# Loading the prompt rows by feature columns and the first weight piece in two halves at the start of a decoder step

## The chip, the cores and the metric

The kernel runs on one core of a Trainium2 chip. The metric is the device time of one launch in microseconds. Three runs of the kernel before gave 911.23, 910.31 and 910.13 us, median 910.31 us.

## What is computed

One layer of a decoder for 512 prompt tokens and 8 sample tokens, 1024 features each, all in float32. The first step, which the change touches, is the input projection, a product of all 520 token rows with a weight matrix of 5376 columns; the kernel computes its first 2048 columns (pooling input, keys, memory query, queries) in one stage of its own:

```
z = x @ w_in        # x: 512 prompt rows and 8 sample rows, 1024 features
q, k, v, u, cq, gates = split(z)
```

After it come rotary embedding, windowed attention with sinks, causal pooling, cross-attention into 256 memory tokens, a gated merge, a layer norm, a mixture of 16 experts (top 2 inside the best group of 4) and a second layer norm. None of these is changed.

## The kernel before

The program is written out engine by engine, with semaphores between the engines; every engine runs its instructions in the order of the text. The change and the steps argued on lie in the first 33 us and a little behind them.

**Loads (SP, from L369).** SP issues all early loads on one hardware queue, in this order: the identity matrix (64 KB, 512-byte rows; `id_in`), the prompt rows in four blocks of 128 tokens (L372, each 512 KB with rows of 4 KB; all four count `x_in`), the 8 sample rows (L373, 32 KB, also `x_in`), the first two weight pieces of `wz` (L380, 1 MB each, into `raw[0]` and `raw[1]`, `raw_in`), the memory rows `mtok` (L384, 1 MB, `m_in`), and then the constants, parameters, pooling and router weights (L385 to L390). At L392 and L393 SP waits until all nine transposed tiles are split, then loads the pooling state (L394), and then piece after piece of `wz` into the two `raw` buffers, each as soon as the piece before it in that buffer is split (L397 to L400).

**Transposes (PE, L1020 to L1031).** PE waits for the identity and for all five loads of `x_in` together (L1021). It transposes the sample rows (8 small transposes, L1023, one increment of `xt_ps`), and then for each block `k` of 128 features the four blocks of 128 tokens into PSUM bank `4 + k % 4` (L1030, four transposes of 128 by 128 for each `k`, one increment). From `k` = 4 on it waits until the bank is free again, that is until ACT and DVE have both read it (L1027, L1028).

**Splits (ACT L586 to L608, DVE L1658 to L1679).** A float32 value is split into a high part in the reduced type `fp32r` and a low part. For the activations ACT copies the PSUM bank to `xhi` (L607, 512 columns; L587 for the sample rows), and DVE subtracts it from the bank to give `xlo` (L1677; L1659). For a weight piece ACT copies `raw` to `whi` (L595, 2048 columns) and DVE gives `wlo` (L1669). Both engines do the sample rows first, then `k` = 0 to 3, then the whole weight piece 0, then `k` = 4 to 7, then piece 1.

**Projection (PE, `z_piece` at L1059, `product` at L1033).** A piece of `wz` holds two output tiles of 128 columns (the halves `u` = 0 and 1, 1024 elements of each partition). Each tile takes 48 matmuls of 260 columns: for two token halves and eight feature blocks the three products hi*hi (L1041), lo*hi (L1042) and hi*lo (L1043). `z_piece(0)` waits for `lo_split` 1, the low part of the whole piece, and its first 24 matmuls wait block by block for `xhi` and `xlo` (L1039, L1040). ACT copies each finished tile to `z` (L618 for tile 0, L620 for tile 1), and then splits the piece that has landed in the buffer that is free. There are eight pieces; the transposes of `mtok` come behind the eighth (L1084).

## Time and profile before

| | |
|---|---|
| median of three runs | 910.31 us |
| the profiled execution: device time | 910.77 us |
| its span, first to last instruction | 908.6 us |
| PE busy | 837.1 us (92% of the span) |
| DVE, ACT, POOL busy | 530.1, 434.5, 170.5 us |
| mean granted clock of TensorE | 0.956 |
| first instruction of PE | 9.87 us after the span's start |
| first matmul of the projection | 19.28 us |

The span is counted from the first instruction of any engine, and 2.2 us of the device time lie outside it. The chain of waits follows the instruction that ended last back to what released it; what stands on it set the end. The timeline gives the instructions of one engine in order; what stands in brackets is the time that the engine was idle before and what ended it. "PEclk" is the clock that TensorE was granted, 1.00 being 2.4 GHz and 0.50 being 1.2 GHz. The queue of SP lists the issue of a load, not its arrival.

### The profile page before, as it was taken

To read this page: it belongs to the slowest core of one execution; us is meant where nothing else is said; L and a number is where in the kernel's file an instruction comes from. 1 tells how busy PE (TensorE), PEld (TensorE's weight loads), DVE (VectorE), ACT (ScalarE), POOL (GpSimd) and SP (SyncE) were. 2 spreads that over 40 slices of the span, in tenths; PEclk is the share of its full clock that TensorE was granted. 3 is DMA by queue.
4 is the path that set the end of the run, shared out by engine and by line. 5 is a ranking of instruction groups with operands and counts; after the bars stand their busy time and mean duration, and the time that the engine had idled before them with its cause. 6 is when DMAs were issued, how large, how long until landed. Compare 5 with 4: busy or idle time off the path is not lost.

```text
span 908.6 us, 13893 instructions
## 1 busy us (share of the span) xinstructions
PE 837.1 (92%) x5420; PEld 742.1 (82%) x5420; DVE 530.1 (58%) x710; ACT 434.5 (48%) x575; POOL 170.5 (19%) x147
## 2 busy tenths in 40 slices
PE   4999988898997999999999997599999999999990
PEld 4999977787885989999999776487888888888870
DVE  3122255646346333444443434779999999999976
ACT  4222232556356242233223214267888788788753
POOL 0086013222122100000000055411121112111104
PEclk9999999999899699999999999599999999999995
DMA  7422200831012113222223363899999999999953
GB/s 293 150 93 92 92 24 25 297 144 48 24 48 88 47 42 132 88 87 87 87 87 139 103 206 129 298 413 397 400 402 389 388 401 402 381 396 402 361 142 94
DMA packets 38143, 179.80 MB, mean 198 GB/s; under 512 B 3919, under 2 KB 11759, under 8 KB 23854
## 3 DMA queue, kind: packets, MB, share of 16 engines
q1 hardware_dynamic: 32486, 159.22, 46.0%
q0 software_dynamic: 5600, 19.99, 7.9%
q8 instruction: 26, 0.43, 0.2%
q14 instruction: 15, 0.12, 0.0%
q10 hardware_dynamic: 16, 0.03, 0.0%
HBM read 164.65 MB, written 16.89 MB: 200 GB/s over the span
## 4 chain that ended last, share of the span: by engine, by line
PE 87%; DVE 6%; DMA 3%; ACT 2%; issue 1%; SPq 0%; DVEq 0%; POOL 0%; POOLq 0%; ACTq 0%
PE ps L1164 7%; PE ps L1165 6%; PE ps L1541 6%; PE ps L1166 6%; PE ps L1543 6%; PE ps L1542 6%; PE ps L1041 4%; PE ps L1042 4%; PE ps L1043 4%; PE ps L1568 3%; PE ps L1570 3%; PE ps L1569 3%; PE ps L1180 2%; PE ps L1182 2%; PE ps L1181 2%; PE ps L1529 2%
## 5 line engine op out<-in xcount | busy, mean ns | idle before, releaser
L2030 DVE TENSOR_TENSOR elo<-eraw,ehi 128x2048 fp32r<-128x2048 f32 x96 | 218.0, 2291 | 25.6 <-ACT ehi L880 23.7
L880 ACT ACTIVATE ehi<-eraw 128x2048 fp32r<-128x2048 f32 x96 | 183.0, 1916 | 27.2 <-PE ps L1543 15.9
L1541 PE MATMUL ps<-ehi,xethi 128*128 128x512 f32 x256 | 103.1, 403 | 3.7 <-issue 2.4
L1543 PE MATMUL ps<-elo,xethi 128*128 128x512 f32 x256 | 101.0, 394 | 0.0
L1542 PE MATMUL ps<-ehi,xetlo 128*128 128x512 f32 x256 | 100.9, 394 | 0.0
L1041 PE MATMUL ps<-xhi,whi 128*128 128x260 f32 x256 | 73.2, 286 | 2.4 <-DVE wlo L1669 2.4
L1164 PE MATMUL ps<-xhi,whi 128*128 128x260 f32 x256 | 74.5, 291 | 0.0
L1165 PE MATMUL ps<-xhi,wlo 128*128 128x260 f32 x256 | 74.0, 289 | 0.0
L1166 PE MATMUL ps<-xlo,whi 128*128 128x260 f32 x256 | 73.9, 289 | 0.0
L1042 PE MATMUL ps<-xhi,wlo 128*128 128x260 f32 x256 | 73.0, 285 | 0.0
L1043 PE MATMUL ps<-xlo,whi 128*128 128x260 f32 x256 | 72.7, 284 | 0.0
L1836 DVE TENSOR_TENSOR wlo<-late,whi 128x2048 fp32r<-128x2048 f32 (+1 forms) x16 | 34.5, 2158 | 64.4 <-ACT whi L813 64.4
L1669 DVE TENSOR_TENSOR wlo<-raw,whi 128x2048 fp32r<-128x2048 f32 x11 | 25.7, 2333 | 68.2 <-ACT whi L595 68.2
L1541 PEld LDWEIGHTS ps<-ehi,xethi 128*128 128x128 f32 x256 | 48.8, 191 | 16.7 <-DVE elo L2030 3.8
L2381 POOL TENSOR_TENSOR probs<-probs,stat 128x1024 f32<-128x1024 f32 (+1 forms) x20 | 34.4, 1722 | 129.5 <-DVE stat L1759 129.5
L1543 PEld LDWEIGHTS ps<-elo,xethi 128*128 128x128 f32 x256 | 48.6, 190 | 10.4
L676 ACT ACTIVATE probs<-probs,stat 128x256 f32<-128x256 f32 (+1 forms) x80 | 38.0, 476 | 38.7 <-DVE stat L1742 36.2
L1542 PEld LDWEIGHTS ps<-ehi,xetlo 128*128 128x128 f32 x256 | 48.7, 190 | 9.3
L2426 POOL DMA_INDIRECT f_dram<-yout,dest x14 | 28.7, 2051 | 121.3 <-ACT yout L900 121.3
L1568 PE MATMUL ps<-ehi,hthi 128*128 128x512 f32 x128 | 51.4, 401 | 0.0
L1041 PEld LDWEIGHTS ps<-xhi,whi 128*128 128x128 f32 x256 | 48.9, 191 | 2.7 <-DVE wlo L1669 2.7
L1164 PEld LDWEIGHTS ps<-xhi,whi 128*128 128x128 f32 x256 | 50.1, 196 | 0.3 <-issue 0.3
(370 smaller groups left out, 2069.1 us busy)
## 6 DMA issues: line engine op xcount, KB each, us to landing
eraw<-w_gate_in SPq DMA_DIRECT2D x32, 1024.0 KB, 20.3
eraw<-w_up_in SPq DMA_DIRECT2D x32, 1024.0 KB, 20.5
eraw<-w_down_in SPq DMA_DIRECT2D x32, 1024.0 KB, 22.2
raw<-wz_in SPq DMA_DIRECT2D x8, 1024.0 KB, 5.2
late<-wm_in SPq DMA_DIRECT2D x8, 896.0 KB, 4.4
late<-wm_in SPq DMA_DIRECT2D x8, 704.0 KB, 4.0
fraw<-wm_in SPq DMA_DIRECT2D x8, 512.0 KB, 3.5
late<-wo_in SPq DMA_DIRECT2D x4, 1024.0 KB, 4.9
```

Of the source, the lines that this page charges most:

```text
L880: ac.activation(ehi[s % 3][:, :], eraw[s][:, :], ACT.Copy).then_inc(ehi_ok, 1)
L1041: pe.matmul(out, sh, mh[n], start=start and k == 0, stop=False)
L1042: pe.matmul(out, sl, mh[n], start=False, stop=False)
L1043: last = pe.matmul(out, sh, ml[n], start=False, stop=stop and k == len(parts) - 1)
L1164: pe.matmul(out, cols(whi[s], q), mh, start=start, stop=False)
L1165: pe.matmul(out, cols(wlo[s], q), mh, start=False, stop=False)
L1166: return pe.matmul(out, cols(whi[s], q), ml, start=False, stop=stop)
L1541: pe.matmul(ps[:, bank, :], hi[:, k, :], ehi[s[j]][:, w], start=k == 0, stop=False)
L1542: pe.matmul(ps[:, bank, :], lo[:, k, :], ehi[s[j]][:, w], start=False, stop=False)
L1543: last = pe.matmul(ps[:, bank, :], hi[:, k, :], elo[s[j]][:, w], start=False, stop=k == KD - 1)
L1568: pe.matmul(ps[:, bank + h, :], hi[:, f, :], ehi[s[j]][:, w], start=f == 0, stop=False)
L2030: ve.tensor_tensor(elo[s % 3][:, :], eraw[s][:, :], ehi[s % 3][:, :].bitcast(F32), ALU.subtract)\
```

## The change

SP now loads the prompt rows in four blocks of 256 features for all 512 tokens (`columns`, each 512 KB in rows of 1 KB), each with a semaphore of its own, `x_in[0]` to `x_in[3]`. Behind the first two of them comes the first half of weight piece 0 (512 KB, `first_in`), then the sample rows (which now count `x_in[1]`), then the last two blocks, then the second half of piece 0 (`raw_in[0]`), then piece 1. The load of `mtok` moves behind the wait for the transposes and the load of the pooling state.

PE waits for one block of features ahead of every second `k`; ahead of `k` = 2 it waits for 32 on `x_in[1]`, the block and the sample rows. The sample transposes move from the front to `k` = 4, and so do their splits on ACT and DVE. Both of these engines split the first half of piece 0 ahead of `k` = 2 (1024 columns, `first_hi`, `first_lo`), and the second half behind `k` = 7. `z_piece(0)` waits for `first_lo` ahead of its first tile and for `lo_split` 1 ahead of its second. Two semaphores that nothing used are dropped.

```diff
-id_in, con_in, x_in, m_in = sem("id_in"), sem("con_in"), sem("x_in"), sem("m_in")
+id_in, con_in, m_in = sem("id_in"), sem("con_in"), sem("m_in")
+x_in = [sem(f"x_in{c}") for c in range(4)]
+first_in, first_hi, first_lo = sem("first_in"), sem("first_hi"), sem("first_lo")
...
-    for t in range(NB):
-        sp.dma_start(xtok[:, t, :], xp[:, t, :]).then_inc(x_in, 16)
-    sp.dma_start(xsam[:, :], a["x_sample"]).then_inc(x_in, 16)
+
+    def columns(c):
+
+        cols = slice(c * 2 * P, c * 2 * P + 2 * P)
+        sp.dma_start(xtok[:, :, cols], xp[:, :, cols]).then_inc(x_in[c], 16)
+
+    columns(0)
+    columns(1)
+    sp.dma_start(raw[0][:, 0:D], a["wz"][0, :, 0:D]).then_inc(first_in, 16)
+    sp.dma_start(xsam[:, :], a["x_sample"]).then_inc(x_in[1], 16)
+    columns(2)
+    columns(3)
+    sp.dma_start(raw[0][:, D:PW], a["wz"][0, :, D:PW]).then_inc(raw_in[0], 16)
...
-    for n in range(2):
-        piece(n, a["wz"][n], PW, True)
-    sp.dma_start(mtok[:, :, :], a["mem_prompt"].rearrange("(t p) d -> p t d", p=P)).then_inc(m_in, 16)
+    piece(1, a["wz"][1], PW, True)
...
+    sp.dma_start(mtok[:, :, :], a["mem_prompt"].rearrange("(t p) d -> p t d", p=P)).then_inc(m_in, 16)
...
-    ac.wait_ge(xt_ps, 1)
-    ac.activation(xhi[:, 0:KD * T].rearrange("p (k t) -> p k t", k=KD)[:, :, SEQ:T],
-                  ps[:, 3, 0:KD * NS].rearrange("p (k t) -> p k t", k=KD), ACT.Copy).then_inc(xt_hi, 1)
-
...
+        if k == 2:
+            ac.wait_ge(first_in, 16)
+            ac.activation(whi[0][:, 0:D], raw[0][:, 0:D], ACT.Copy).then_inc(first_hi, 1)
         if k == 4:
-            split(0, 0, PW, 16, True)
-        ac.wait_ge(xt_ps, k + 2)
+            ac.wait_ge(xt_ps, 5)
+            ac.activation(xhi[:, 0:KD * T].rearrange("p (k t) -> p k t", k=KD)[:, :, SEQ:T],
+                          ps[:, 3, 0:KD * NS].rearrange("p (k t) -> p k t", k=KD), ACT.Copy).then_inc(xt_hi, 1)
+        ac.wait_ge(xt_ps, k + 1 + k // 4)
         ac.activation(xhi[:, k * T:k * T + SEQ], ps[:, 4 + k % 4, :], ACT.Copy).then_inc(xt_hi, 1)
+    ac.wait_ge(raw_in[0], 16)
+    ac.activation(whi[0][:, D:PW], raw[0][:, D:PW], ACT.Copy).then_inc(hi_split, 1)
...
-    pe.wait_ge(x_in, 16 * (NB + 1))
     for k in range(KD):
-        last = pe.transpose(ps[:, 3, k * NS:k * NS + NS], xsam[:, k * P:k * P + P], ident[0:NS, 0:NS])
-    last.then_inc(xt_ps, 1)
-    for k in range(KD):
+        if k % 2 == 0:
+            pe.wait_ge(x_in[k // 2], 32 if k == 2 else 16)
+        if k == 4:
+            for j in range(KD):
+                last = pe.transpose(ps[:, 3, j * NS:j * NS + NS], xsam[:, j * P:j * P + P], ident[0:NS, 0:NS])
+            last.then_inc(xt_ps, 1)
         if k >= 4:
-            pe.wait_ge(xt_hi, k - 2)
-            pe.wait_ge(xt_lo, k - 2)
+            pe.wait_ge(xt_hi, k - 3)
+            pe.wait_ge(xt_lo, k - 3)
...
-                    pe.wait_ge(xt_hi, k + 2)
-                    pe.wait_ge(xt_lo, k + 2)
+                    pe.wait_ge(xt_hi, k + 1 + k // 4)
+                    pe.wait_ge(xt_lo, k + 1 + k // 4)
...
-        pe.wait_ge(lo_split, n + 1)
+        if first:
+            pe.wait_ge(first_lo, 1)
+        else:
+            pe.wait_ge(lo_split, n + 1)
         for u in range(2):
+            if first and u:
+                pe.wait_ge(lo_split, 1)
...
-    ve.wait_ge(xt_hi, 1)
-    ve.tensor_tensor(xlo[:, 0:KD * T].rearrange("p (k t) -> p k t", k=KD)[:, :, SEQ:T],
-                     ps[:, 3, 0:KD * NS].rearrange("p (k t) -> p k t", k=KD),
-                     xhi[:, 0:KD * T].rearrange("p (k t) -> p k t", k=KD)[:, :, SEQ:T].bitcast(F32),
-                     ALU.subtract).then_inc(xt_lo, 1)
-
...
+        if k == 2:
+            ve.wait_ge(first_hi, 1)
+            ve.tensor_tensor(wlo[0][:, 0:D], raw[0][:, 0:D], whi[0][:, 0:D].bitcast(F32), ALU.subtract)\
+              .then_inc(first_lo, 1)
         if k == 4:
-            split(0, 0, PW, True)
-        ve.wait_ge(xt_hi, k + 2)
+            ve.wait_ge(xt_hi, 5)
+            ve.tensor_tensor(xlo[:, 0:KD * T].rearrange("p (k t) -> p k t", k=KD)[:, :, SEQ:T],
+                             ps[:, 3, 0:KD * NS].rearrange("p (k t) -> p k t", k=KD),
+                             xhi[:, 0:KD * T].rearrange("p (k t) -> p k t", k=KD)[:, :, SEQ:T].bitcast(F32),
+                             ALU.subtract).then_inc(xt_lo, 1)
+        ve.wait_ge(xt_hi, k + 1 + k // 4)
         ve.tensor_tensor(xlo[:, k * T:k * T + SEQ], ps[:, 4 + k % 4, :], xhi[:, k * T:k * T + SEQ].bitcast(F32),
                          ALU.subtract).then_inc(xt_lo, 1)
+    ve.wait_ge(hi_split, 1)
+    ve.tensor_tensor(wlo[0][:, D:PW], raw[0][:, D:PW], whi[0][:, D:PW].bitcast(F32), ALU.subtract)\
+      .then_inc(lo_split, 1)
```

## Rows read from the trace of the kernel before

**Rows 1.** the page: shares of the chain that ended last, by engine
```profile
PE 87%; DVE 6%; DMA 3%; ACT 2%; issue 1%; SPq 0%; DVEq 0%; POOL 0%; POOLq 0%; ACTq 0%
```

**Rows 2.** the chain of waits, 0 to 27 us: start us, duration us, what
```profile
3.07 6.67 DMA xsam<-x_sample_in
...
9.87 0.99 PE ps L1023 x8
10.86 3.62 PE ps L1030 x16
...
14.50 0.60 ACT xhi L607
15.10 1.81 ACT whi L595
...
16.93 2.30 DVE wlo L1669
...
19.28 0.59 PE ps L1041
```

**Rows 3.** waits of PE, whole execution: total us, times, longest us
```profile
PE ps L1023 <- DMA xsam<-x_sample_in: 9.9, 1, 9.9
...
PE ps L1502 <- DVE both L2060: 5.1, 1, 5.1
...
PE ps L1041 <- DVE wlo L1669: 2.4, 1, 2.4
```

**Rows 4.** timeline of ACT, 0 to 120 us: start, busy us, instruction, idle before
```profile
26.76 0.60 ACT L618 ACTIVATE z<-ps 128x520 f32<-128x520 f32 x1 [6.10 <-PE ps L1043]
32.50 0.60 ACT L620 ACTIVATE z<-ps 128x520 f32<-128x520 f32 x1 [5.14 <-PE ps L1043]
33.00 1.91 ACT L595 ACTIVATE whi<-raw 128x2048 fp32r<-128x2048 f32 x1
```

**Rows 5.** timeline of DVE, the same stretch
```profile
13.43 0.69 DVE L1677 TENSOR_TENSOR xlo<-ps,xhi 128x512 fp32r<-128x512 f32 x1 [0.16 <-ACT xhi L607]
...
16.93 2.29 DVE L1669 TENSOR_TENSOR wlo<-raw,whi 128x2048 fp32r<-128x2048 f32 x1 [1.11 <-ACT whi L595]
```

**Rows 6.** timeline of SP's queue, the same stretch
```profile
1.18 1.84 SPq L372 DMA_DIRECT2D xtok<-x_prompt_in  x4
...
3.56 0.82 SPq L380 DMA_DIRECT2D raw<-wz_in  x2
```

**Rows 7.** windows: stretch, PE, PEld, DVE, ACT, POOL busy, then PEclk, DMA share, GB/s
```profile
0.00:2.00 2.00, 0.00 (x0) 0.00 (x0) 0.00 (x0) 1.28 (x1) 0.73 (x8) 1.00 0.07 16
2.00:3.00 1.00, 0.00 (x0) 0.00 (x0) 0.00 (x0) 0.00 (x0) 0.00 (x0) 1.00 0.65 152
3.00:4.00 1.00, 0.00 (x0) 0.00 (x0) 0.00 (x0) 0.00 (x0) 0.00 (x0) 1.00 0.93 307
4.00:8.20 4.20, 0.00 (x0) 0.00 (x0) 0.00 (x0) 0.00 (x0) 0.00 (x0) 1.00 1.06 423
15.30:16.85 1.55, 1.55 (x13) 1.32 (x11) 0.53 (x1) 1.55 (x2) 0.00 (x0) 1.00 1.07 432
19.10:22.40 3.30, 3.12 (x14) 3.12 (x15) 3.30 (x6) 1.55 (x1) 0.00 (x0) 0.50 0.09 23
165.00:173.00 8.00, 8.00 (x67) 7.07 (x66) 4.01 (x20) 4.71 (x21) 1.47 (x2) 1.00 1.05 352
```

**Rows 8.** tile raw, 0 to 15 us: the two loads of L380, issue to landing
```profile
DMA to landing us min/median/max: 8.4/9.5/10.5
```

**Rows 9.** tile cach_k, 190 to 200 us: the two loads of L423, issue to landing
```profile
DMA to landing us min/median/max: 4.0/4.5/5.0
```

**Rows 10.** the chain of waits at 113 us: sixteen transposes of L1084
```profile
113.34 1.75 PE ps L1084 x16
```

**Rows 11.** windows further on, same columns as rows 7
```profile
220.00:250.00 30.00, 28.39 (x196) 24.96 (x194) 13.03 (x51) 13.34 (x43) 3.97 (x3) 0.83 0.12 36
290.00:320.00 30.00, 28.03 (x174) 25.77 (x174) 11.05 (x16) 10.38 (x33) 3.79 (x2) 0.66 0.19 67
```

More of the change, by code:

```diff
@@ L274, in decoder_step @@
             "h_ps", "h_sum", "h_stat", "h_root", "h_fac", "h_nrm", "h_gain", "h_done", "h_last", "h_sent"))
-        ht_ps, ht_out, lg_ps, lg_out = sem("ht_ps"), sem("ht_out"), sem("lg_ps"), sem("lg_out")
+        ht_ps, ht_out, lg_ps = sem("ht_ps"), sem("ht_out"), sem("lg_ps")
         rc_in, rd, gd_ok, dist_ok, r_exp, both_ok, rank_ps, list_ok, over_ok = (sem(n) for n in (
@@ L283, in decoder_step @@
         xe_in, y_sent = [sem(f"xe_in{q}") for q in range(2)], sem("y_sent")
-        g_ps, sig_ok, act_ok, hid_ok, hidt_ps, hidt_hi, hidt_lo = (sem(n) for n in (
-            "g_ps", "sig_ok", "act_ok", "hid_ok", "hidt_ps", "hidt_hi", "hidt_lo"))
+        sig_ok, act_ok, hid_ok, hidt_ps, hidt_hi, hidt_lo = (sem(n) for n in (
+            "sig_ok", "act_ok", "hid_ok", "hidt_ps", "hidt_hi", "hidt_lo"))
         y_out, moe_done = sem("y_out"), sem("moe_done")
```

## The prediction

> **What bounds the kernel now.** I read the shares of the chain first: PE carries 87% of it [rows 1], so anything that lets PE begin its projection earlier, without making it idle later, should shorten the run one for one. Next I read the beginning of that chain [rows 2]. The reader should see a strictly serial start. The landing of the sample rows holds it until 9.74 us, since PE waits for all five loads together. Eight small transposes (0.99) and sixteen of the 32 large ones (3.62) follow; then the chain leaves PE and goes through ACT (the fourth copy, then the high part of weight piece 0, 1.81) and DVE (its low part, 2.30), and comes back at 19.28 us for the first matmul of the projection. The waits of PE say the same [rows 3]: 9.9 us for the loads, and 2.4 us between its last transpose and the low part of piece 0. This start is where the change acts. The queue's timeline [rows 6] shows that the loads are issued long before their data move: the two weight pieces are issued from 3.56 to 4.38 us, while the first weight piece lands 8.4 us after its issue, at 3.56 + 8.4 = 12.0 us, and the second 10.5 us after its own (last of L380, issued near 4.0), at 14.5 us [rows 6, 8]. So the queue is limited by bytes, and the order of the loads decides when each arrives.
>
> **When the loads land.** The windows [rows 7] give 16 GB/s up to 2 us, 152 from 2 to 3, 307 from 3 to 4, and 423 from there on, so 0.49 MB have moved by 4.0 us. Identity, prompt and sample rows are 2.20 MB, moved by 4.0 + 1.71/0.423 = 8.0 us, and the last landing is seen at 9.74 [rows 2]; the same sum puts the two weight pieces at about 11.0 and 13.5 against landings at 12.0 and 14.5. From the last byte to the semaphore it takes 1.0 to 1.7 us; I take 1.3. The new prompt loads have rows of 1 KB. A stretch in which the loads of the caches with such rows ran shows 352 GB/s [rows 7], so I take that for the four column blocks, 1.49 us for each 0.524 MB, and 423 for the half pieces, 1.24 us. Landings by this: block 0 at 4.3 + 1.3 = 5.6, block 1 at 7.1, first half piece 8.3, sample rows 8.4 (8.8 with the lag of 1.7 that they have now), block 2 at 9.9, block 3 at 11.4, second half piece 12.6, piece 1 at 15.1. The two bounds: at 423 throughout the last block is 1.0 us earlier, and at 307 it is about 0.9 later.
>
> A page bears on this. The Trainium skill, "DMA: Bandwidth & Descriptors", section "Anatomy of one DMA — SWDGE (gpsimd) path", gives a load a fixed 2.0 us beside its bytes at 436 GB/s. That would be an estimate of 1.18 + 2.0 + 1.35 = 4.5 us for block 0 with the identity in front. The row of 152 GB/s contradicts so quick a start, and the sum above goes by the row.
>
> **The new schedule, step by step.** A block k of four transposes costs 3.62/4 = 0.9 us at the rate that the chain shows at 10.86 us [rows 2], and 1.75/4 = 0.44 later on [rows 10]. The granted clock is recorded as 1.00 in both places, yet 13 matmuls pass in the 1.55 us from 15.3, 0.12 us each [rows 7], so I read the first stretch as the lower level (1.2 GHz) and take the rise at about 15.3 us, 5.4 us after PE began. If PE begins at 5.7, the same distance gives 11.1 us.
> - k = 0 and 1: 5.7 to 7.5. k = 2 needs block 1 and also the sample rows, which stand behind the half piece: 8.6. So PE idles 1.1 us and does k = 2 and 3 until 10.4.
> - ACT, idle anyway, copies k = 0 and 1 and takes the first half piece at 8.4 to 9.4 (half of 1.81, and a little); DVE gives its low part from 9.4 to 10.6 (half of 2.29 [rows 5]). These 1.0 and 1.2 us were 1.81 and 2.30 on the chain; now they lie beside transposes. Then k = 2 and 3: `xlo` is ready at 11.3 and 12.0, at 0.69 each [rows 5].
> - Sample transposes 10.4 to 11.4; k = 4 to 7 at 0.44 to 0.9 each, with block 3 there at 11.4. With a rise at 12.5 (the idle 1.1 us may delay it) they end at 12.2, 12.8, 13.2 and 13.7. The bank of k = 7 is free at 12.0, so that wait costs nothing; if `xlo` of k = 3 came after 13.2 it would be what is late next.
> - First matmul: 13.6 us, against 19.28. It takes 0.36 us for each k, so k = 7 is wanted at 16.1, while ACT and DVE have it by 15.2. Earliest end of the bounds: 12.6 (loads at 423, clock risen before k = 4). Latest: 15.0, all 32 transposes at 0.9.
> - Second half piece: ACT 14.6 to 15.6, DVE 15.6 to 16.8; wanted at 13.6 + 5.74 = 19.3 (the half piece at full rate, from the two copies at 26.76 and 32.50 [rows 4]). Covered by 2.5 us; if the cover is gone, each microsecond late is one on PE. Piece 1: high part 15.6 to 17.5, low part 17.5 to 19.8, wanted at 25.1. Covered too.
> - The added waits on SP are none. `mtok` moves behind L392; queued behind it is the load of the third `wz` piece. The queue should run dry near 17.6, state rows and `mtok` (1.3 MB) take 3.1 us more, and the third piece lands near 24.5. ACT takes it today at 33.00 [rows 4], which becomes 26; so it costs nothing, and even 6 us late it would still be split before PE needs it. `mtok` itself is used at 113 us [rows 10]. The one extra issue (about 0.41 us, half of the 0.82 for two [rows 6]) runs ahead of the data, as the others do now.
> - Clock: PE today has only 14 matmuls in the 3.3 us from 19.1, at a granted 0.50 [rows 7]. 3.12/14 = 0.22 us each against 5.74/48 = 0.12: 1.3 us. PE fell to 1.2 GHz there after 2.2 us of standing still. In the new order it has no pause above 1.1 us before the matmuls, so I count these 1.3 us as gained.
>
> Sum: 19.28 - 13.6 + 1.3 = 7.0 us. Everything behind the first matmul hangs on PE and on buffers that it frees, so it moves as a whole. Against the profiled execution's 910.77 us that is 903.8; the median of the runs stands 0.46 below that execution, so I forecast 903.3 us. Bounds of the likeliest case: start 12.6 gives 8.0, start 15.0 with the clock already risen gives 5.6, so 902.3 to 904.7; and later stretches at half clock (below) can move it by one more or one less, 1.6 us.
>
> **The rivals.**
> *The clock stays low.* The pauses of the new start (one of 1.1 us, perhaps another behind k = 3) keep PE at 1.2 GHz through all the transposes, and the first 14 matmuls are slow as before. Start 15.0, gain 4.3, time 906.0. For it: today the rise took 5.4 us of work without a pause. Against: the work before the matmuls is now spread over 9 us. The Trainium skill, "TensorE: Matmul & The Clock Gate", Part 1, says that the throttled state is the default, that activity lifts it, and that the number of slow matmuls varies from run to run. By that rule this rival and my case could both be seen in runs of one kernel; no run here has shown that. 18%.
>
> *Gained at the start, lost further on.* PE runs at half clock again in 220 to 250 us (mean granted clock 0.83) and 290 to 320 (0.66) [rows 11], so 0.17 x 60 + 0.34 x 60 = 31 us at 1.2 GHz. These follow PE's waits, the longest of them 5.1 us for DVE [rows 3]. If the shift changes how the pauses fall, each further stretch like the one from 19.1 us costs 1.6 us. Three more: 908.1. Against: nothing in those stretches is edited. 10%.
>
> *The loads come one after another: slower.* Two loads of 0.5 MB in 1 KB rows at 192 us landed 4.0 and 5.0 us after their issues [rows 9]. If five such loads did not overlap, at 4.0 each from 1.18 us, block 3 would land at 21.2, the first matmul would start at 22.2, 2.9 us later than now, and the time would be 913.2. It decides from a landing of block 3 at 18.3 us (3.4 us for each load). Against it: those two landed 1.4 us apart, and today's loads move 423 GB/s together. The Trainium skill, "DMA: Bandwidth & Descriptors", section "Bandwidth", asks for loads of at least 1 MiB to reach 75% of the peak, which speaks against cutting; by its fixed cost and rate the estimate is 3.2 us a load and 17.2 us for block 3. 4%.
>
> *It does not do what it says.* PE waits for k = 2 on the sample rows and for k = 4 on block 2; should the small load come last of all, as it does today, near 12 us, the transposes would bunch behind it and start late: k = 2 to 7 and the samples from 12 at 0.9 each, start 18.4, gain 0.9 + 1.3, time 908.1. 3%.
>
> **How the numbers follow.** My case has 65%. The range takes in the first rival: 900.9 to 906.6. A difference of 0.2% (1.8 us) is about what a measurement of this kernel can tell from none. Faster by more than that: my case, the first rival, most of the second, 0.92. Within it: 0.03. Slower: 0.05.
>
> **What would show it.** In the profile after, PE's first instruction stands near 5.7 us with an `xtok` block as its releaser; the first projection matmul near 13.6, with no wait for a weight's low part ahead of it; ACT's copy of the second tile near 25.5 instead of 32.50; 360 GB/s or so from 4 to 8 us. The stretches of [rows 11] come 7 us earlier with the same clocks. It is wrong if the first matmul waits for a half piece, if block 3 lands after 13, or if the copy of the second tile is early by 7 us and the end is not.

## The result, and the profile after

The changed kernel took 906.18 us in the median of five runs (905.56 to 906.89), against 910.31 us for the kernel before. The ratio is 0.9944, with a 95% interval of 0.9921 to 0.9967: faster by 4.1 us in the medians. The ratio is worked out from all the runs, except two of the kernel before in later groups that fell into a slower state (975.89 and 2114.46 us), and not from the two medians, whose quotient is 0.9955; a second group of the same two kernels (below) gave 0.9954, so the gain is 4.1 to 5.1 us. The forecast was 903.3 with a range of 900.9 to 906.6. Sign and range held; the size was 7.0 us forecast against 4.1. The median is outside the 902.3 to 904.7 of the likeliest case, and inside the range only because the range takes in the first rival. The profiled execution took 906.89 us, so it stands 3.9 us below the profiled execution of before: 3.5 of it in the span (905.0 against 908.6), 0.4 outside it (1.8 us of the device time lie outside the span, 2.2 before).

The page of the changed kernel, its span, busy times and shares of the chain, which answer to [rows 1]:

```profile
span 905.0 us, 13896 instructions
...
PE 838.0 (93%) x5420; PEld 742.2 (82%) x5420; DVE 529.9 (59%) x711; ACT 435.3 (48%) x576; POOL 170.3 (19%) x147
...
PE 87%; DVE 6%; DMA 3%; ACT 2%; issue 2%; SPq 0%; DVEq 0%; POOL 0%; POOLq 0%; ACTq 0%
```

PE carries the same 87% of the chain. The chain of waits at the start, which answers to [rows 2] (start us, duration us, what):

```profile
3.17 8.37 DMA xtok<-x_prompt_in
11.59 1.02 PE ps L1040 x8
12.61 3.34 PE ps L1046 x16
15.95 0.12 PE ps L1057
```

Of the six links that stood ahead of the first matmul only three are left: the landing of a column block at 11.54, the sample transposes, and sixteen large transposes. ACT and DVE are gone from it; their work on the weight (now 1.06 and 1.23 us, for the half piece) lies beside the transposes. But the block that the chain waits for is not the last of five loads at 9.74; it is block 2 at 11.54, later than all of x came before. PE's timeline up to its first projection matmul:

```profile
5.35 1.94 PE L1046 MATMUL ps<-con,xtok 128*128 128x128 f32 x8 [5.35 <-DMA xtok<-x_prompt_in]
9.33 1.97 PE L1046 MATMUL ps<-con,xtok 128*128 128x128 f32 x8 [2.04 <-DMA xsam<-x_sample_in]
11.59 1.02 PE L1040 MATMUL ps<-con,xsam 8*128 8x8 f32 x8 [0.29 <-DMA xtok<-x_prompt_in]
12.54 3.41 PE L1046 MATMUL ps<-con,xtok 128*128 128x128 f32 x16
15.71 0.37 PE L1057 MATMUL ps<-xhi,whi 128*128 128x260 f32 x1
```

Three things are to be seen. PE begins at 5.35 us (forecast 5.7). It pauses for 2.04 us ahead of k = 2, for the sample rows. And the last sixteen transposes take 3.41 us, 0.85 for each k, so PE was at the slow rate until about 15.6 us; the trace's first entry of the granted clock, 1.00, begins at 15.55. From the first projection matmul at 15.71 on there is none of the slow stretch of before. ACT's timeline, which answers to [rows 4]:

```profile
10.10 1.06 ACT L613 ACTIVATE whi<-raw 128x1024 fp32r<-128x1024 f32 x1 [2.17 <-DMA raw<-wz_in]
...
21.74 0.61 ACT L632 ACTIVATE z<-ps 128x520 f32<-128x520 f32 x1 [2.39 <-PE ps L1059]
27.48 0.61 ACT L634 ACTIVATE z<-ps 128x520 f32<-128x520 f32 x1 [5.14 <-PE ps L1059]
28.32 1.92 ACT L602 ACTIVATE whi<-raw 128x2048 fp32r<-128x2048 f32 x1 [0.23 <-DMA raw<-wz_in]
```

The second tile's copy stands at 27.48 us instead of 32.50: the start gained 5.02 us. This copy is the mark by which the starts are compared below, since it includes the slow matmuls where there are any. The copy of the third piece's high part waited 0.23 us for its load. Windows, which answer to [rows 7] and, in the last line, show a stretch behind the start (columns as there):

```profile
4.00:8.00 4.00, 1.94 (x8) 1.57 (x8) 0.73 (x2) 1.19 (x2) 0.00 (x0) 1.00 0.94 261
19.10:22.40 3.30, 3.30 (x30) 3.30 (x29) 2.29 (x1) 0.85 (x2) 0.00 (x0) 1.00 1.04 320
118.00:121.30 3.30, 3.30 (x17) 3.30 (x16) 2.29 (x1) 0.18 (x1) 0.00 (x0) 0.50 0.03 5
```

From 4 to 8 us the queue moved 261 GB/s where it moved 421 before and 352 was forecast. From 19.1 to 22.4 us PE had 30 matmuls at a granted clock of 1.00, where it had 14 at 0.50. And there is a new stretch at 0.50, from 118 to 121.3 us, with 17 matmuls. The loads of the prompt blocks, from issue to landing (tile `xtok`, 0 to 16 us; the middle one is block 2, issued at 3.17 us, the last one block 3, issued at 3.60):

```profile
DMA to landing us min/median/max: 4.0/8.4/9.4
```

So block 2 landed at 11.55 and block 3 at 13.03. PE's waits, which answer to [rows 3]:

```profile
PE ps L1046 <- DMA xtok<-x_prompt_in: 5.4, 1, 5.4
PE ps L1523 <- DVE both L2086: 5.1, 1, 5.1
...
PE ps L1046 <- DMA xsam<-x_sample_in: 2.0, 1, 2.0
```

The wait of 9.9 us has become 5.4 and 2.0, with 0.3 more ahead of the sample transposes; the 2.4 us for the low part is gone. The wait of 5.1 us further on has not changed.

### The profile page after: what moved, and what is told of

It reads as the page before. It is cut to its first block, busy times and chain, and to the rows that moved or that the text cites. A ratio compares the mean times of both kernels' runs of the same rounds, so it can differ in the third digit from the quotient of the medians.

```text
span 905.0 us, 13896 instructions
## 1 busy us (share of the span) xinstructions
PE 838.0 (93%) x5420; PEld 742.2 (82%) x5420; DVE 529.9 (59%) x711; ACT 435.3 (48%) x576; POOL 170.3 (19%) x147
## 4 chain that ended last, share of the span: by engine, by line
PE 87%; DVE 6%; DMA 3%; ACT 2%; issue 2%; SPq 0%; DVEq 0%; POOL 0%; POOLq 0%; ACTq 0%
PE ps L1185 7%; PE ps L1186 6%; PE ps L1562 6%; PE ps L1187 6%; PE ps L1564 6%; PE ps L1563 6%; PE ps L1057 4%; PE ps L1058 4%; PE ps L1059 4%; PE ps L1589 3%; PE ps L1591 3%; PE ps L1590 3%; PE ps L1201 2%; PE ps L1203 2%; PE ps L1202 2%; PE ps L1550 2%
## 5 line engine op out<-in xcount | busy, mean ns | idle before, releaser
L1684 DVE TENSOR_TENSOR wlo<-raw,whi 128x2048 fp32r<-128x2048 f32 x10 | 23.5, 2347 | 64.7 <-ACT whi L602 64.7
L2452 POOL DMA_INDIRECT f_dram<-yout,dest x14 | 28.7, 2050 | 121.3 <-ACT yout L914 121.3
L1185 PEld LDWEIGHTS ps<-xhi,whi 128*128 128x128 f32 x256 | 50.0, 195 | 0.3 <-issue 0.3
L1186 PEld LDWEIGHTS ps<-xhi,wlo 128*128 128x128 f32 x256 | 50.0, 195 | 0.0
```

Source lines behind the costliest of these rows:

```text
L1185: pe.matmul(out, cols(whi[s], q), mh, start=start, stop=False)
L1186: pe.matmul(out, cols(wlo[s], q), mh, start=False, stop=False)
```

## The experiments

All kernels of a group ran on one chip beside runs of the kernel before. There are four groups, and the kernel before had medians of 910.31 (changed), 910.62 (halves only to memory rows back), 911.25 (changed once more, both kinds of rows, idle transposes 12, 9) and 910.85 us (the others). Times of single runs of one kernel differ by 3 us and more, so each row gives the ratio with its interval. The mark is the end of the start: ACT's second copy in the profiled execution. "Half clock" is the time for which PE was granted 1.2 GHz between 110 and 330 us, read off windows of 1 us. "Clock rose" is where the trace's first entry of the granted clock begins. Until then the transposes of each trace take 0.42 us each, and behind it 0.27 until the clock falls again.

| kernel | median us | ratio (95%) | second copy, us | gain at the mark | profiled run, gain at the end | half clock, us | clock rose, us |
|---|---|---|---|---|---|---|---|
| before | 910.31 | | 32.50 | | | 30.7 | 15.7 |
| changed | 906.18 | 0.9944 (0.9921 to 0.9967) | 27.48 | 5.0 | 3.9 | 34.1 | 15.6 |
| changed, once more | 907.01 | 0.9954 (0.9939 to 0.9969) | 27.76 | 4.7 | 3.5 | 34.1 | 15.8 |
| halves only | 908.50 | 0.9973 (0.9955 to 0.9990) | 28.17 | 4.3 | 5.4 | 30.7 | 14.1 |
| columns only | 911.09 | 1.0012 (0.9998 to 1.0026) | 32.52 | 0.0 | -0.9 | 34.2 | 13.3 |
| samples early | 906.69 | 0.9956 (0.9941 to 0.9970) | 28.15 | 4.4 | 2.3 | 37.5 | 17.3 |
| memory rows back | 906.80 | 0.9963 (0.9951 to 0.9975) | 27.82 | 4.7 | 5.7 | 30.7 | 17.2 |
| rows of 4 KB | 906.55 | 0.9942 (0.9920 to 0.9965) | 27.45 | 5.1 | 3.3 | 37.5 | 16.3 |
| rows of 1 KB, contiguous | 907.09 | 0.9951 (0.9932 to 0.9970) | 27.32 | 5.2 | 3.6 | 34.1 | 15.7 |
| idle transposes 12, 9 | 904.43 | 0.9930 (0.9907 to 0.9953) | 27.02 | 5.5 | 3.3 | 37.6 | 5.8 |
| before, pause filled | 910.86 | 0.9999 (0.9984 to 1.0014) | 30.87 | 1.6 | -1.0 | 37.5 | 16.5 |
| samples by ACT's queue | 905.66 | 0.9940 (0.9916 to 0.9964) | 27.99 | 4.5 | 5.7 | 30.7 | 17.2 |
| idle transposes 12, 16, 13 | 904.91 | 0.9936 (0.9919 to 0.9953) | 25.30 | 7.2 | 5.8 | 34.2 | 6.6 |
| all together | 903.42 | 0.9919 (0.9902 to 0.9935) | 25.54 | 7.0 | 7.4 | 30.8 | 8.8 |

### Each part by itself

**Halves only.** The prompt rows come by tokens again and are waited for together; the two half pieces stay. The sample rows and the first half piece move behind the four prompt blocks (not shown).

```diff
-                sp.dma_start(xtok[:, :, cols], xp[:, :, cols]).then_inc(x_in[c], 16)
+                sp.dma_start(xtok[:, c, :], xp[:, c, :]).then_inc(x_in[c], 16)
...
-                if k % 2 == 0:
-                    pe.wait_ge(x_in[k // 2], 32 if k == 2 else 16)
+                if k == 0:
+                    for c in range(4):
+                        pe.wait_ge(x_in[c], 32 if c == 1 else 16)
```

> The changed kernel with the prompt rows loaded by tokens again, all five loads waited for together; the two halves of weight piece 0 and everything else stay as changed. Theory A (the halves did the work, by ending PE's pause of 2.4 us ahead of the first matmul; the column loads brought PE's first transposes forward but at 1.2 GHz): first transpose at 9.9 us, first matmul near 16.7, no half-rate stretch behind it, the second tile's copy near 28.5 us (27.48 in the changed kernel, 32.50 before), time about 907 us. Rival (the column loads brought most of it): first matmul above 18 us, time about 909.5 us.

PE's timeline of this kernel:

```profile
9.89 3.65 PE L1046 MATMUL ps<-con,xtok 128*128 128x128 f32 x16 [9.89 <-DMA xsam<-x_sample_in]
13.47 0.90 PE L1040 MATMUL ps<-con,xsam 8*128 8x8 f32 x8
14.30 2.34 PE L1046 MATMUL ps<-con,xtok 128*128 128x128 f32 x16
16.40 0.37 PE L1057 MATMUL ps<-xhi,whi 128*128 128x260 f32 x1
```

PE starts 4.5 us later than in the changed kernel and is ready for the projection only 0.7 us later, at 16.40. The last sixteen transposes take 2.34 us and not 3.41, because the clock had risen at 14.1 us, just ahead of them. The second copy is at 28.17. So at the mark the halves alone bring 4.3 of the 5.0 us, as theory A had it (28.5 expected). In the times they bring less, 0.9973, with a median of 908.50 us where 907 was expected; the profiled execution was the fastest of its ten runs. On the same chip the kernels with samples early and with the memory rows back, which have the column loads too, took 906.69 and 906.80 us, 1.7 to 1.8 us less, though their marks are at most 0.4 us earlier. So the mark does not tell the whole share of the column loads, and no run here shows where the rest comes from.

**Columns only.** Piece 0 arrives and is split whole, behind k = 7 (of the edit only the loads are shown; ACT, DVE and PE lose the half piece's splits and waits).

```diff
-            sp.dma_start(raw[0][:, 0:D], a["wz"][0, :, 0:D]).then_inc(first_in, 16)
             sp.dma_start(xsam[:, :], a["x_sample"]).then_inc(x_in[1], 16)
             columns(2)
             columns(3)
-            sp.dma_start(raw[0][:, D:PW], a["wz"][0, :, D:PW]).then_inc(raw_in[0], 16)
+            sp.dma_start(raw[0][:, 0:PW], a["wz"][0]).then_inc(raw_in[0], 16)
```

> The changed kernel with weight piece 0 loaded and split whole, behind the eighth block of prompt features; the loads by feature columns stay. Theory A: transposes end near 15.9 us as in the changed kernel, then PE waits for the whole piece (high part 1.9 us, low part 2.3 us) until about 20 us, its clock falls to 1.2 GHz in that pause, and the time is 910 to 911 us, no gain. Rival (column loads bring most of the gain): first matmul below 18 us, time about 907 us.

```profile
5.19 3.66 PE L1042 MATMUL ps<-con,xtok 128*128 128x128 f32 x16 [5.19 <-DMA xtok<-x_prompt_in]
...
10.18 3.46 PE L1042 MATMUL ps<-con,xtok 128*128 128x128 f32 x16
18.46 0.58 PE L1053 MATMUL ps<-xhi,whi 128*128 128x260 f32 x1 [4.81 <-DVE wlo L1690]
```

That is its timeline of PE. The transposes end at 13.6 us, even earlier than in the changed kernel, since no half piece stands ahead of block 2. PE then stands still for 4.8 us for the low part of the whole piece. Its first matmul is at 18.46, 0.8 us before the one of before, but slow; the second copy, 32.52, is where it was. By themselves the column loads bring nothing (1.0012), as expected. They are worth something only beside the halves: 0.7 us at the mark, and 1.7 us in the medians of one chip (above). The first matmul at 18.46 was expected near 20. The clock rose only at 13.3 us here, 8.1 us after PE's first work, with one pause of 0.4 us in between; before it had been 5.8 us.

### What held the start back

**Samples early.** The sample rows are issued ahead of the half piece, and PE waits for them only at k = 4.

```diff
+            sp.dma_start(xsam[:, :], a["x_sample"]).then_inc(x_in[2], 16)
             sp.dma_start(raw[0][:, 0:D], a["wz"][0, :, 0:D]).then_inc(first_in, 16)
-            sp.dma_start(xsam[:, :], a["x_sample"]).then_inc(x_in[1], 16)
...
-                    pe.wait_ge(x_in[k // 2], 32 if k == 2 else 16)
+                    pe.wait_ge(x_in[k // 2], 32 if k == 4 else 16)
```

> The changed kernel with the sample rows issued ahead of the first half piece and waited for only at their own transposes, not ahead of k = 2. Theory A (block 2 of the columns, landing near 11.5 us, and the low clock set the end of the transposes): PE's pause of 2.0 us at 7.3 us goes, a pause of about 2 us ahead of block 2 takes its place, transposes end near 15.9 us, time within 0.5 us of the changed kernel. Rival (the wait for the sample rows was the loss): transposes end 1 to 2 us earlier and the time falls by as much.

```profile
5.56 3.65 PE L1046 MATMUL ps<-con,xtok 128*128 128x128 f32 x16 [5.56 <-DMA xtok<-x_prompt_in]
11.35 1.02 PE L1040 MATMUL ps<-con,xsam 8*128 8x8 f32 x8 [2.15 <-DMA xtok<-x_prompt_in]
12.30 3.67 PE L1046 MATMUL ps<-con,xtok 128*128 128x128 f32 x16
```

PE's timeline: the pause of 2.0 us at 7.3 us is gone, and 2.15 us stand ahead of block 2 in its place; the transposes end at 15.97, as they did. Beside the first profile of the changed kernel the wait for the sample rows cost nothing by itself: block 2 came no earlier. In the second profile it did cost: the sample rows let k = 2 begin only at 9.98, PE was busy with k = 3 until the sample transposes at 11.88, and block 2 had landed at 11.28, 0.6 us before.

**Memory rows back** in their old place behind piece 1.

```diff
             piece(1, a["wz"][1], PW, True)
+            sp.dma_start(mtok[:, :, :], a["mem_prompt"].rearrange("(t p) d -> p t d", p=P)).then_inc(m_in, 16)
...
-            sp.dma_start(mtok[:, :, :], a["mem_prompt"].rearrange("(t p) d -> p t d", p=P)).then_inc(m_in, 16)
```

> The changed kernel with the load of the memory rows back in its old place, behind piece 1. Theory (the move costs and brings nothing on PE): first matmul 15.7 us, second copy 27.5 us, third weight piece high part starts at 28.0 instead of 28.32, time within 0.3 us. Rival (moving it freed bytes for something on PE's path): time up by 0.5 us or more.

```profile
22.08 0.60 ACT L632 ACTIVATE z<-ps 128x520 f32<-128x520 f32 x1 [3.18 <-PE ps L1059]
27.82 0.61 ACT L634 ACTIVATE z<-ps 128x520 f32<-128x520 f32 x1 [5.14 <-PE ps L1059]
28.33 1.91 ACT L602 ACTIVATE whi<-raw 128x2048 fp32r<-128x2048 f32 x1
```

ACT's timeline: the copy of the third piece follows the tile's copy without the 0.23 us wait; nothing on PE's path changes. The ratio, 0.9963, is inside the first interval of the changed kernel. Moving the memory rows costs and brings nothing that these runs can tell.

**Rows of 4 KB**, and **rows of 1 KB, contiguous**: the same blocks out of memory that was laid out by block.

```diff
-                sp.dma_start(xtok[:, :, cols], xp[:, :, cols]).then_inc(x_in[c], 16)
+                sp.dma_start(xtok[:, c, :], a["x_cols"][c]).then_inc(x_in[c], 16)
```

```diff
-                sp.dma_start(xtok[:, :, cols], xp[:, :, cols]).then_inc(x_in[c], 16)
+                sp.dma_start(xtok[:, :, cols], a["x_cols"][c].rearrange("(t p) d -> p t d", p=P)).then_inc(x_in[c], 16)
```

> The changed kernel with the prompt rows laid out in memory beforehand so that each column block is one contiguous 512 KB area and arrives in 128 rows of 4 KB; order, sizes and waits as changed. Theory B (rows of 1 KB out of lines of 4 KB arrive slowly, which is why block 2 came at 11.5 us and not at 9.9): 400 GB/s or more from 4 to 8 us instead of 261, k = 2 starts before 8.6 us (9.33), the sample transposes at about 10.0 (11.59), transposes end near 14.4 (15.95), second copy near 26.2 us (27.48), time 1 to 1.5 us below the changed kernel. Rival (the queue is slow at the start for another reason): all of these as in the changed kernel.

> As the kernel with 4 KB rows, each column block one contiguous 512 KB area, but still in rows of 1 KB as the changed kernel has them. If the distance of 4 KB between the rows' starts is what slows them, this is as fast as the 4 KB rows (above 380 GB/s from 4 to 8 us, sample transposes near 10.0 us). If the length of the rows is, it is as slow as the changed kernel (about 260 GB/s, sample transposes at 11.5 us).

The window from 4 to 8 us, first with rows of 4 KB, then with contiguous rows of 1 KB (columns as [rows 7]; the last is GB/s):

```profile
4.00:8.00 4.00, 1.94 (x8) 1.57 (x8) 0.89 (x2) 1.19 (x2) 0.00 (x0) 1.00 0.98 326
```

```profile
4.00:8.00 4.00, 1.94 (x8) 1.57 (x8) 0.38 (x1) 0.76 (x2) 0.00 (x0) 1.00 0.98 299
```

326 and 299 GB/s, where the changed kernel had 261 and, in its second profile, 289. Neither reaches the 400 of theory B. But the landings did move. With rows of 4 KB, issue to landing of the prompt blocks (block 2 is the middle one, issued at 3.02, block 3 the last, issued at 3.41):

```profile
DMA to landing us min/median/max: 3.9/7.0/7.9
```

| kernel | first half piece | block 2 | block 3, us |
|---|---|---|---|
| changed, two profiles | 10.07, 9.27 | 11.55, 11.28 | 13.03, 12.76 |
| five others with rows of 1 KB out of lines of 4 KB | 8.52 to 9.78 | 10.05 to 11.31 | 11.53 to 12.79 |
| rows of 1 KB, contiguous | 9.17 | 10.71 | 12.35 |
| rows of 4 KB; all together | 8.53; 8.38 | 10.04; 9.78 | 11.33; 11.06 |

With rows of 4 KB block 2 landed at 10.04, as theory B had it (10.0), and block 3 earlier than in any profile with rows of 1 KB and a half piece ahead of it, by 0.2 to 1.7 us. Contiguous rows of 1 KB lie among the others. So the length of the rows seems to be worth about 1 us here and the distance between them nothing, with one or two profiles for each; theory B held for the landings and failed for the rate. PE made nothing of it: k = 2 still had to wait for the sample rows until 8.96, k = 3 kept PE busy until the sample transposes at 10.85 (10.0 expected), and the clock rose only at 16.3 us, so that the last sixteen transposes took 3.67 us. The second copy came at 27.45, where 26.2 was expected.

**Samples by ACT's queue.** The last candidate was the small load of eight rows within SP's queue.

```diff
         def _(ac):
+            ac.dma_start(xsam[:, :], a["x_sample"]).then_inc(x_in[2], 16)
```

> The changed kernel with the load of the sample rows issued from ACT's queue at the start and waited for only at its own transposes. Theory E (the small load of 8 rows within SP's queue is what holds the bytes back at 6 to 8 us): above 380 GB/s from 4 to 8 us instead of 261 to 289, block 2 and with it the sample transposes near 10.0 us. Rival (the dip comes with the strided 1 KB and 4 KB rows, or with the start in general): still below 320 GB/s and block 2 after 10.8 us; time as the changed kernel.

It moved 290 GB/s from 4 to 8 us, and the sample transposes began at 11.17, when block 2 had landed (11.13). Theory E fell. For comparison, the kernel with halves only, whose prompt rows come by tokens (windows 4 to 8 and 8 to 10 us):

```profile
4.00:8.00 4.00, 0.00 (x0) 0.00 (x0) 0.00 (x0) 0.00 (x0) 0.00 (x0) 1.00 1.03 415
8.00:10.00 2.00, 0.11 (x1) 0.14 (x2) 0.00 (x0) 0.00 (x0) 0.00 (x0) 1.00 1.01 293
```

415 GB/s, and a dip of its own from 8 to 10 us, when the prompt rows are through. Its first half piece, behind the same number of bytes as block 3 in the kernels above, landed at 10.72. What slows the queue near the fifth to eighth microsecond in every kernel with column blocks stays open.

### The clock

**Idle transposes.** PE transposes the identity into an unused bank while it waits; the results are not used. First 12 ahead of block 0 and 9 ahead of block 1:

```diff
                 if k % 2 == 0:
+                    for _ in range(12 if k == 0 else 9 if k == 2 else 0 if k == 4 else 0):
+                        pe.transpose(ps[:, 0, 0:P], ident, ident)
```

> The changed kernel with 12 idle transposes of the identity on PE ahead of its wait for block 0 and 9 ahead of its wait for block 1 and the sample rows, so that PE has no pause in 2.7 to 11.5 us; their results are not used. Theory C (the pauses of the new start keep PE at 1.2 GHz through all 32 transposes): the rise comes before 12 us, the last sixteen transposes take about 2 us instead of 3.41 and end near 14.1 us, when the low part of k = 3 frees the bank for k = 7; second copy near 25.9 us; time 1.5 us below the changed kernel. Rival (the rate of these transposes is not a matter of the clock's history): no change, or slower where the idle transposes run into the first real ones.

```profile
8.54 1.09 PE L1048 MATMUL ps<-con,xtok 128*128 128x128 f32 x8 [0.96 <-DMA xsam<-x_sample_in]
11.33 0.66 PE L1042 MATMUL ps<-con,xsam 8*128 8x8 f32 x8 [1.69 <-DMA xtok<-x_prompt_in]
11.92 3.00 PE L1048 MATMUL ps<-con,xtok 128*128 128x128 f32 x16
```

PE's timeline: k = 2 and 3 now take 1.09 us, the fast rate. Then PE pauses 1.69 us ahead of block 2, its clock falls at 12.7 us, and the last sixteen transposes take 3.00 us. The expectation held in its first half only. The six times lay in two groups (902.5, 902.5, 902.9 and 906.0, 907.2, 907.5), which led to the next kernel, with 12, 16 and 13 ahead of blocks 0, 1 and 2, so that this pause is filled too.

```diff
-                    for _ in range(12 if k == 0 else 9 if k == 2 else 0 if k == 4 else 0):
+                    for _ in range(12 if k == 0 else 16 if k == 2 else 13 if k == 4 else 0):
```

> The changed kernel with idle transposes ahead of three waits of PE: 12 ahead of block 0, 16 ahead of block 1 and the sample rows, 13 ahead of block 2. The kernel with 12 and 9 still had a pause of 1.7 us ahead of block 2, its clock fell at 12.7 us in the profiled execution, and its times fell into two groups, near 902.5 and near 906.5. Theory C (that pause decides which): no fall before 20 us, the last sixteen transposes in 2.1 us, first matmul near 13.8, second copy near 25.5 us, all times near 902.5 to 904.5. Rival: two groups of times again.

```profile
9.70 1.58 PE L1038 MATMUL ps<-con 128*128 128x128 f32 x13
11.22 0.66 PE L1042 MATMUL ps<-con,xsam 8*128 8x8 f32 x8
11.80 1.97 PE L1048 MATMUL ps<-con,xtok 128*128 128x128 f32 x16
13.53 0.37 PE L1059 MATMUL ps<-xhi,whi 128*128 128x260 f32 x1
```

```profile
25.30 0.61 ACT L634 ACTIVATE z<-ps 128x520 f32<-128x520 f32 x1 [5.14 <-PE ps L1061]
```

PE's timeline and one line of ACT's: the sample transposes take 0.66 us and the last sixteen 1.97 instead of 3.41. The first projection matmul is at 13.53 us and the second copy at 25.30: 7.2 us gained at the mark, 2.2 more than the changed kernel. Of these 2.2 us, 1.8 are the clock (from the sample transposes to the first matmul 2.31 us instead of 4.12) and 0.4 the earlier sample transposes. They were not held back by a load:

```profile
DMA to landing us min/median/max: 4.1/6.9/7.9
```

Block 2, issued at 3.17, landed at 10.05; what kept PE until 11.2 us were the 13 idle transposes themselves. The times (902.9 to 906.1) did not fall into two groups, but the median, 904.91, is above the 902.5 to 904.5 expected, and the ratio, 0.9936, is not clear of the changed kernel's two, 0.9944 and 0.9954.

**Before, pause filled.** Twenty idle transposes in the 2.4 us pause of the kernel before measure what its slow matmuls cost.

```diff
+            for _ in range(20):
+                pe.transpose(ps[:, 0, 0:P], ident, ident)
             z_piece(0, 0, True)
```

> The kernel before with 20 idle transposes of the identity on PE between the last prompt transpose and the first projection matmul, where it stands still for 2.4 us; their results are not used. Clock theory: no fall at 19.1 us, the first 14 matmuls at 0.12 us each, second copy near 31.1 us instead of 32.50, time 1.3 us below before: 909. It measures by itself the 1.3 us that the prediction counted for the clock. Rival: the slow matmuls have another cause, no change or slower.

```profile
17.01 2.35 PE L1069 MATMUL ps<-con 128*128 128x128 f32 x20
19.11 0.36 PE L1041 MATMUL ps<-xhi,whi 128*128 128x260 f32 x1
```

```profile
30.87 0.60 ACT L620 ACTIVATE z<-ps 128x520 f32<-128x520 f32 x1 [5.14 <-PE ps L1043]
```

The first matmul is at 19.11 (its loads landed 0.2 us earlier) and the second copy at 30.87, 1.6 us earlier than before: 0.2 for the loads and 1.4 to 1.5 for the clock (from the first matmul to the second copy 11.76 us instead of 13.22), against 1.3 in the forecast. But the twelve runs show nothing of it: 0.9999 (0.9984 to 1.0014), where 909 us was expected, and the profiled execution even ended 1.0 us later. What a start gains is not yet what the run gains.

**Changed, once more.** The same program a second time.

> The changed kernel once more, unedited, beside the others. Theory D (the start gains 5.0 us every time; what is lost or won behind it comes from where PE's clock happens to fall, which differs between executions of one program): the second copy again near 27.5 us within 0.7, but the falls of the clock behind 100 us in other places than at 118, 220, 231, 241 and 289 us, and the span differs from 905.0 by up to 3 us. Rival (the fall at 118 us is caused by the shift): a fall at 118 us again.

The second copy stood at 27.76 and the span was 905.4 us. The clock fell at 118.2, 220.6, 230.8, 241.1, 288.9 and 312.8 us, the same places as in the first profile within 0.3 us, so the expectation of other places failed here and its rival seemed right. The kernel with the memory rows moved back, whose start has the same order and whose mark is 0.3 us later, decides it. Windows of the kernel before, of the changed kernel, and of that one (the column behind POOL's is the granted clock):

```profile
110.00:170.00 60.00, 51.48 (x339) 45.07 (x338) 33.06 (x66) 17.64 (x40) 15.08 (x12) 1.00 0.19 62
200.00:330.00 130.00, 121.04 (x909) 105.95 (x909) 58.53 (x184) 60.82 (x193) 24.79 (x14) 0.88 0.14 45
```

```profile
110.00:170.00 60.00, 51.49 (x323) 44.86 (x323) 34.08 (x73) 19.89 (x50) 15.08 (x12) 0.97 0.25 78
200.00:330.00 130.00, 120.67 (x904) 105.44 (x903) 60.68 (x184) 58.95 (x184) 24.82 (x14) 0.88 0.14 45
```

```profile
110.00:170.00 60.00, 52.62 (x333) 45.22 (x331) 33.90 (x75) 21.20 (x51) 15.11 (x12) 0.97 0.24 75
```

All three have a pause of PE of 2.8 us in the same step, the one ahead of the values' product. The mark and DVE's first work on the product behind the pause (126.51 us before, 123.01 changed, 121.83 with the memory rows back) show what it did: at the mark the changed kernel was 5.0 us ahead, behind the pause 3.5; the kernel with the memory rows back was 4.7 us ahead in both places. In the kernel of before the pause (119.7 to 122.5 us) went without a fall; in the changed kernel (114.7 to 117.5) the clock fell at 118.0. With the memory rows back there was no fall there, but one at 153.7 us. So a pause of this kind may or may not bring a fall, and it is not the change's shift alone that decides.

**All together**: blocks contiguous in rows of 4 KB, the samples by ACT's queue, and 12, 8 and 14 idle transposes.

```diff
-                sp.dma_start(xtok[:, :, cols], xp[:, :, cols]).then_inc(x_in[c], 16)
+                sp.dma_start(xtok[:, c, :], a["x_cols"][c]).then_inc(x_in[c], 16)
...
+            ac.dma_start(xsam[:, :], a["x_sample"]).then_inc(x_in[2], 16)
...
-                    pe.wait_ge(x_in[k // 2], 32 if k == 2 else 16)
+                    for _ in range(12 if k == 0 else 8 if k == 2 else 14 if k == 4 else 0):
+                        pe.transpose(ps[:, 0, 0:P], ident, ident)
+                    pe.wait_ge(x_in[k // 2], 32 if k == 4 else 16)
```

> All that helped the start in one kernel: column blocks contiguous in memory in rows of 4 KB, the sample rows by ACT's queue, and 12, 8 and 14 idle transposes ahead of blocks 0, 1 and 2. If the loads (B, E) and the clock (C) are independent losses: block 2 near 10.0 us, first matmul near 13.2 us (ACT and DVE, with their half piece, are then what is late), second copy near 25.0 us, time about 902.5, the forecast's schedule. Rival (the clock alone counts): as the kernel with idle transposes and no other edit.

The first matmul is at 13.76, the second copy at 25.54, the sample transposes at 11.46 (here the identity landed late, at 3.05 us). The prompt blocks, issue to landing (blocks 0, 1 and 3, the last issued at 3.18):

```profile
DMA to landing us min/median/max: 4.1/4.9/7.9
```

Block 1 was there at 6.54 and block 3 at 11.06; the last increment of block 2's semaphore is at 9.78, as expected (10.0). But eight idle transposes held PE until k = 2 at 8.96, and fourteen until the sample transposes at 11.46. The median is 903.42 and the ratio 0.9919 (0.9902 to 0.9935), the best of all. At the mark it was no faster than the kernel with idle transposes alone (25.54 against 25.30), as the rival had it. The reason is not that earlier loads are worth nothing: the idle transposes were counted for the old landings and filled the time that the loads had gained, in both kernels. What earlier loads bring at the fast clock, with fewer idle transposes, was not run. The intervals of the two ratios overlap.

## Why the prediction was right, and where it was off

**The mechanism was right.** The start was a serial chain, the change broke it, and what PE gained it carried on. The low part of the weight is off the chain; the second half piece and piece 1 were in time (PE worked without a pause from 15.71 us to the end of piece 0); no wait of 2.4 us came back. That the 14 slow matmuls behind PE's pause cost 1.3 us was right, too, at the mark: 1.4 to 1.5 measured, and none of them is in the changed kernel's two profiles. In the run times that term by itself is not shown: with the pause filled the kernel before was no faster. Of the 5.0 us at the mark 3.6 are the earlier first matmul (5.7 forecast) and 1.4 this term.

**Two terms of the new schedule were mis-sized, and together they cost the 2.1 us between 13.6 and 15.71.** The first is the loads. The queue moved 261 GB/s from 4 to 8 us where I had taken 352. The sample rows let k = 2 begin at 9.33 instead of 8.6, and with block 2 at 11.54 instead of 9.9 the sample transposes began at 11.59 instead of 10.4: 1.2 us. The second is the rise of the clock. I took the distance of before, 5.4 us from PE's first work (5.8 by the trace's first entry), and put the rise at 12.5 us. It came at 15.6, though PE began 4.5 us earlier. From the sample transposes to the first matmul it took 4.1 us where I had counted 3.2: 0.9 us. That distance was no fixed quantity to carry over: without pauses above 0.4 us it was 4.2 (halves only), 5.8 and 6.9 (before, and with its pause filled, where the same instructions run up to there) and 8.1 us (columns only), and 3.2 to 5.7 in the kernels with idle transposes; in the kernels with the pauses of the new start 9.9 to 12.0.

The kernel with all pauses filled shows what the second term weighs: the samples and the last sixteen took 0.66 and 1.97 us. Its first matmul at 13.53 us and its gain of 7.2 us at the mark are the forecast's 13.6 and 7.0, but that agreement is luck in part: the clock rose at 6.6 us, much earlier than the 12.5 of the forecast, because 12 idle transposes ran from 2.67 us on, and the sample transposes began at 11.2 instead of 10.4, held by idle transposes. What the first term weighs beside a fast clock stays open.

This is close to the first rival, the transposes slow throughout: 906.0 us at 18%, and the measured time is 906.18. It came true but for the first matmuls, which were fast in both profiles, and the start was at 15.7 instead of 15.0. That the times agree to 0.2 us is luck: its gain of 4.3 us was to stand at the start, where 5.0 were measured, and of these the medians kept 4.1. In other kernels (samples early, memory rows back, samples by ACT's queue) the first matmuls were slow as well, with marks at 27.8 to 28.2. By the Trainium skill, "TensorE: Matmul & The Clock Gate", Part 1, that number varies from run to run. The two profiles of the changed kernel, each without a slow matmul, do not show this. What bears it out is the moment of the rise: 15.7 and 16.5 us in the two profiles in which the instructions up to there are those of the kernel before.

The sentence that I had set aside, a fixed 2.0 us and the bytes at 436 GB/s from the Trainium skill, "DMA: Bandwidth & Descriptors", section "Anatomy of one DMA — SWDGE (gpsimd) path", gave an estimate of 4.5 us for block 0; the section's figure is for loads that GpSimd issues, and these are issued by SP. The block landed at 5.22 and 4.87 us in two profiles of the changed kernel, 0.4 to 0.7 later than that, and PE used it at 5.35 and 5.01, 0.3 to 0.7 earlier than my 5.7.

**The order of worth was not forecast.** The forecast let PE's early start and the shorter wait work as one. The runs part them: halves alone 4.3 us at the mark, columns alone 0.0, both 5.0 and 4.7. In the medians beside their own runs of before the halves alone brought 2.1 us and both 4.1 and 4.2.

**Of the second rival some came true.** It said that gains at the start can be lost to further falls of the clock at 1.6 us each. In the profiled pair one more stretch of 3.4 us at half clock took back 1.5 us at 118 us. Over the whole table, profiled runs with 30.7 us of half clock ended up to 1.2 us better than their mark (four kernels, the last with 0.5), those with about 34.1 us 0.9 to 1.6 us worse, and those with 37.5 us 1.7 to 2.7 us worse. That the median gain is 4.1 us and not the 5.0 of the mark fits this, but with one profile for each kernel the share of it is argued, not shown, and by the ratio of the first group the gain was 5.1.

The slower rival (loads one after another) did not happen: block 3 was there before its turn. The third piece landed near 28.3 us, not 24.5, because SP's wait for the second half's low part ended at 18.8 and not 16.8; the cover was nearly used up (0.23 us for ACT), and PE did not notice.

## What to carry to other kernels

When a start is a chain of load, transpose, split and product, find the piece that the first product waits for and cut it: loads in a finer order brought nothing while the whole weight piece stood behind them, and something as soon as it was halved. Before counting an earlier start at its full length, ask at which clock the early work runs and what pauses lie in it; here 41 idle transposes in the pauses were worth 2.2 us at the start, while the run times do not yet tell that kernel from the changed one. And read a load's arrival from its landing, not from the work that uses it: PE can be busy, or kept busy by idle work, when the load is long there. Where the same program's runs differ by 3 us, judge a start by a mark in the profile behind it, and the kernel by its runs; the two need not agree.

## What was not expected of the hardware

- Column blocks arrive slower than the same bytes by tokens: 261 to 337 GB/s from 4 to 8 us in all kernels with blocks, 397 to 421 in those with token rows. Contiguous memory and rows of 4 KB (326) did not cure it, though with them block 3 landed at 11.33 and 11.06 us, against 11.53 to 13.03 with rows of 1 KB; neither did another queue for the small load (290).
- PE's clock rose near 15.6 us both when its first work was at 9.87 us and when it was at 5.35 us with a pause of 2.0 us in between; with first work between 5.2 and 5.9 us and such pauses it rose at 15.6 to 17.3 us. In the kernel with 12 and 9 idle transposes it fell again at 12.7 us, after a pause of 1.69 us.
- The windows show a granted clock of 1.00 from the start of the span, though the transposes until 15 us take 0.42 us each, as they do at 0.50 in the kernel with 12 and 9 idle transposes (from 12.7 us on). The trace of the changed kernel has no entry of the clock before 15.55 us; what the windows show ahead of the first entry says nothing.
- The time at half clock between 110 and 330 us was 30.7 to 37.6 us for programs that do the same work there.
